# Input loads ahead of weights, half of the squares' sum on GpSimd, and an earlier sigmoid table

## The chip, the core and the metric

One core of a Trainium2 chip runs the whole program. TensorE (PE) multiplies matrices into PSUM, VectorE (DVE), ScalarE (ACT) and GpSimd (POOL) work on elements, and SyncE (SP) issues the DMA loads and stores. Each engine takes its instructions in the order written, and semaphores order the engines among each other. The metric is the device time of one execution in microseconds, the median of several runs. Before the change it is 633.22 us (three runs, 632.15 to 635.92).

## The reference

Two layers of a streaming encoder over 544 positions (512 of a prompt, 32 of a sample with a past). In layer 0 the input x is normalised by its root mean square, projected, gated and convolved:

```
u = x * rsqrt(mean(x*x) + eps) * g_pre
a, gl, z = split(u @ w_in, 3);  v = a * sigmoid(gl)
y = silu(layernorm(depthwise_conv(v, 31 taps)))
h = x + rmsnorm((y * silu(z)) @ w_out) * g_post
```

Layer 1 is a latent attention (low-rank q, a shared latent for keys and values, 16 heads, block-causal mask), again gated and projected. Everything is float32. The kernel reaches float32 accuracy in its projections with three matmuls per product: each operand is split into a rounded high part and the low rest, and high x high, high x low and low x high are summed.

The change touches only the start of layer 0: the loads, the norm of x, and the ScalarE table for the first sigmoid.

## The kernel before

**Layout.** x is held as xT: 1024 channels in 8 tiles of 128 partitions, 544 positions as columns. The columns are two halves of 272, called half 0 and half 1 (`blk(0)`, `blk(1)`). "Tile n" is channel tile n mod 8 of half n div 8, so there are 16 of them.

**Loads.** SP issues x in four quarters (half 0 in two, half 1 in two), each of 4 channel tiles, and the weights in units of 128 x 384 through a ring of 5 stage buffers. Unit u + 5 is loaded once GpSimd has finished unit u (`lo_done`).

**Weights.** ScalarE rounds a unit to its high part (`hi`, L406), and GpSimd subtracts it to get the low part (`lo`, L412).

**The norm, half by half.** ScalarE squares x into y, two tiles at a time (`xsquare`, L515). VectorE adds the eight square tiles up in four folds (`xfold`, L854): three of two tiles each, a last one of a single tile. TensorE multiplies by ones to sum over the partitions (`xstat`, L1429). VectorE makes the variance (L860), ScalarE the root (`sqrt_of`, L521), VectorE the reciprocal (L871).

**The scaled tiles.** For n = 0 to 15 VectorE writes x * g * reciprocal into PSUM (L911, semaphore `u_full`), ScalarE rounds it to the high part (L537, `uhi_done`), and VectorE subtracts for the low part (L892, `u_lo`), one tile behind. The program puts the folds of half 1 into this loop at n = 0 and n = 1, its variance at n = 6 and its reciprocal at n = 8.

**The first products.** TensorE takes tile n as soon as its low part is there: six matmuls (gate and value columns, three each; L421 to L423). The sum for half 1 stands in its stream in front of the products of tile 4. After tile 15 ScalarE takes the sigmoid of the gate columns (L592); TensorE's next group, 48 matmuls, writes into the same PSUM banks and waits for it. Then VectorE multiplies value and sigmoid (`glu`, L927 and L928) and works off the taps of the convolution (L952 to L957), one channel group j after another. The second `glu`, for j = 1, stands among the taps of j = 0 and needs the second group of TensorE matmuls of j = 1.

**Tables.** ScalarE holds one table of functions at a time. The first instruction loads the one with the square root. The next load before the change is the one that the first sigmoid needs, and it stands right in front of it.

The order of all this is fixed by the order in which each engine's program is written; no scheduler moves anything.

Of the kernel before, what the change touches and what calls it, by code (L numbers as in the profile page):

```python
# [196 lines left out]
def build(nc, x_t, state_t, ckv_t, ckr_t, w_in, w_ao, w_kv, w_bi, w_qb, w_kb, w_bo, vecs_d, cc_d, ss_d, krs_d,  # L197
          y_out, conv_out, c_out, kr_out):
    ctx = ExitStack()
    with ctx:  # L200
        def sem(name):
            return ctx.enter_context(nc.semaphore(name))
# [101 lines left out]
        tap_done, y_ready = sem("tap_done"), sem("y_ready")  # L304
        ln_norm, yz_full = sem("ln_norm"), sem("yz_full")
        h_done, xn_full, xn_lo_dve = sem("h_done"), sem("xn_full"), sem("xn_lo_dve")
        xsum_done = sem("xsum_done")
        osum_done, hsum_done, qsum_done, fsum_done = sem("osum_done"), sem("hsum_done"), sem("qsum_done"), sem("fsum_done")
        kr_done, c_full, qn_full = sem("kr_done"), sem("c_full"), sem("qn_full")
        g_evac_dve, rope_done, max_done, prob_done, pt_evac_dve, att_done = (  # L310
# [15 lines left out]
        def blk(b):  # L326
            return slice(b * HB, (b + 1) * HB)
# [104 lines left out]
        def _(sp):  # L432
# [5 lines left out]
            for i in range(4):  # L438
                b, k = i // 2, KD // 2 * (i % 2)
                sp.dma_start(xT[:, k:k + KD // 2, blk(b)], x_t[:, k:k + KD // 2, blk(b)]).then_inc(x_in[i], 16)  # L440
                if i == 1:
                    for u in range(3):
                        load(u)
            sp.dma_start(vecs[:], vecs_d).then_inc(vecs_in, 16)
            for u in range(3, 8):
                load(u)
            sp.dma_start(state[:], state_t).then_inc(state_in, 16)
            for j in range(KD):
# [55 lines left out]
        def _(act):  # L504
# [19 lines left out]
                xsquare(n)  # L524
            hi(act, 0)
            hi(act, 1)
            sqrt_of(N_IN, 0)
            xsquare(4)
            xsquare(5)
            hi(act, 2)  # L530
            hi(act, 3)
            xsquare(6)
            xsquare(7)
            for n in range(2 * KD):
                b, k = divmod(n, KD)
                act.wait_ge(u_full, n + 1)
                nc.scalar.activation(act_hi[:, k, blk(b)], ps[:, 6 + n % 2, 0:HB], ACT.Copy).then_inc(uhi_done, 1)  # L537
                if n < 4:
                    hi(act, 4 + n)
                if n >= KD:  # L540
                    hi(act, n)
                if n == 6:
                    sqrt_of(N_IN + 1, 1)

            def ysquare(j):

# [290 lines left out]
        def _(dve):  # L837
# [34 lines left out]
                dve.wait_ge(rstd_done, n + 1)  # L872


            def xfold(b, i):

                if i < 4:
                    fold(y[:, 0:2, blk(b)], y[:, 2 * i:2 * i + 2, blk(b)], xsq_done, 4 * b + i + 1, xsum_done,
                         4 * b + i - 1 if i > 1 else 0)
                else:  # L880
                    fold(y[:, 0, blk(b)], y[:, 1, blk(b)], xsq_done, 4 * b + 4, xsum_done, 4 * b + 3)

            for i in range(1, 5):
                xfold(0, i)
            dve.wait_ge(xstat_done, 1)
            variance(N_IN, ps[:, 4, 0:HB], D, 0)
            inverse(N_IN, None, 0)
# [7 lines left out]
            dve.wait_ge(vecs_in, 16)  # L895
            for n in range(2 * KD):
                b, k = divmod(n, KD)
                if n == 0:
                    xfold(1, 1)
                    xfold(1, 2)  # L900
                if n == 1:
                    xfold(1, 3)
                    xfold(1, 4)
                if n == 6:
                    dve.wait_ge(xstat_done, 2)
                    variance(N_IN + 1, ps[:, 5, 0:HB], D, 1)
                if n == KD:
                    inverse(N_IN + 1, None, 1)
                if n >= 2:
                    dve.wait_ge(u_lo, n - 1)  # L910
                nc.vector.scalar_tensor_tensor(out=ps[:, 6 + n % 2, 0:HB], in0=xT[:, k, blk(b)],  # L911
                                               scalar=vecs[:, V_PRE0 + k:V_PRE0 + k + 1],
                                               in1=stat(N_IN + b), op0=ALU.mult, op1=ALU.mult).then_inc(u_full, 1)
                if n:
                    u_split(n - 1)
# [356 lines left out]
        def _(pool):  # L1272
            nc.gpsimd.memset(eye, 0.0).then_inc(pool_set, 1)
            pool.wait_ge(pool_set, 1)
            nc.gpsimd.affine_select(out=eye, in_=eye, compare_op=ALU.not_equal, fill=1.0, base=0,
                                    pattern=[[-1, P]], channel_multiplier=1).then_inc(pool_set, 1)
            for u in range(2 * KD):
                lo(pool, u)

            def tap_add(j, i):  # L1280

# [136 lines left out]
        def _(pe):  # L1418
# [6 lines left out]
            pe.wait_ge(const_set, 1)  # L1425

            def xstat(b):
                pe.wait_ge(xsum_done, 4 * (b + 1))
                nc.tensor.matmul(ps[:, 4 + b, 0:HB], ones[:], y[:, 0, blk(b)], start=True, stop=True).then_inc(xstat_done, 1)  # L1429

            xstat(0)
# [1 line left out]
            for j in range(KD):  # L1433
                if j == 0:
                    for b in range(NB):
                        for k in range(KD):
                            if b == 0:
                                ready(pe, k)
                                if k == 4:
                                    xstat(1)  # L1440
                            pe.wait_ge(u_lo, KD * b + k + 1)
                            for t in range(2):
                                last = mm3(half_of(t, b), cols(slot(k), P * t), act_hi[:, k, blk(b)],
                                           act_lo[:, k, blk(b)], k == 0, k == KD - 1)
                                if b and k == KD - 1:
                                    last.then_inc(mt_done, 1)
# [373 lines left out]
```

## Time and profile before

| what | us |
|---|---|
| median of 3 runs | 633.22 (632.15 to 635.92) |
| profiled execution | 633.14 |
| its span | 631.4 |
| TensorE busy | 545.7 (86%) |
| VectorE busy | 451.3 (71%) |
| ScalarE busy | 306.8 (49%) |
| GpSimd busy | 298.2 (47%) |

The profiled execution is told by the device; the span is the time from the first to the last instruction that the profile shows, so 1.74 us lie outside it. Busy shares are means over stages with different limits: which engine sets the pace is seen from the table by stages and from what ended each wait.

### The profile page before, as it was taken

To read this page: it belongs to the slowest core of one execution; us is meant where nothing else is said; L and a number is where in the kernel's file an instruction comes from. 1 tells how busy PE (TensorE), PEld (TensorE's weight loads), DVE (VectorE), ACT (ScalarE), POOL (GpSimd) and SP (SyncE) were. 2 spreads that over 40 slices of the span, in tenths; PEclk is the share of its full clock that TensorE was granted. 3 is DMA by queue.
4 is the path that set the end of the run, shared out by engine and by line. 5 is a ranking of instruction groups with operands and counts; after the bars stand their busy time and mean duration, and the time that the engine had idled before them with its cause. 6 is when DMAs were issued, how large, how long until landed. Compare 5 with 4: busy or idle time off the path is not lost.

```text
span 631.4 us, 10827 instructions
## 1 busy us (share of the span) xinstructions
PE 545.7 (86%) x4044; PEld 497.4 (79%) x4044; DVE 451.3 (71%) x855; ACT 306.8 (49%) x730; POOL 298.2 (47%) x271
## 2 busy tenths in 40 slices
PE   0699999999983669998999998998999999779981
PEld 0699999988952669987999997777777777469980
DVE  4887999999987994888758122856867868850066
ACT  5454665365646773655336325355454554444230
POOL 3349878898894770473647731102111112205033
PEclk9999999999997689999999999999999999959996
DMA  7233133222430310332133222020030031101003
GB/s 239 82 104 89 52 103 90 79 76 66 136 86 1 103 31 28 88 95 67 34 101 105 95 83 57 15 72 17 13 91 2 17 120 36 49 17 51 2 30 112
DMA packets 31397, 43.17 MB, mean 68 GB/s; under 512 B 5840, under 2 KB 21744, under 8 KB 31344
## 3 DMA queue, kind: packets, MB, share of 16 engines
q1 hardware_dynamic: 31344, 42.47, 23.2%
q8 instruction: 32, 0.52, 0.4%
q14 instruction: 21, 0.17, 0.1%
HBM read 37.25 MB, written 3.10 MB: 64 GB/s over the span
## 4 chain that ended last, share of the span: by engine, by line
PE 42%; DVE 36%; ACT 6%; issue 5%; POOL 4%; SPq 3%; DMA 3%; DVEq 0%; ACTq 0%; POOLq 0%
DVE ps L957 13%; PE ps L421 10%; PE ps L423 9%; PE ps L422 9%; PE ps L1636 3%; PE ps L1677 2%; DVE probs L1209 2%; POOL part L1288 2%; DVE y L1002 2%; PE ps L1657 2%; DVE ps L871 2%; SPq L484 2%; ACT probs L787 2%; POOL rlow_lo L412 1%; DVE y L854 1%
## 5 line engine op out<-in xcount | busy, mean ns | idle before, releaser
L412 POOL TENSOR_TENSOR rlow_lo<-stage,rlow_hi 128x384 fp32r<-128x384 f32 (+2 forms) x88 | 99.6, 1141 | 215.8 <-ACT rlow_hi L406 215.8
L421 PE MATMUL ps<-act_hi,rlow_hi 128*128 128x272 f32 (+1 forms) x368 | 110.7, 301 | 22.0 <-POOL act_lo L1341 9.3
L957 DVE SCALAR_TENSOR_TENSOR ps<-v,vecs,ps 128x574 f32<-128x574 f32 x165 | 120.6, 814 | 0.0
L421 PE MATMUL ps<-act_hi,rtop_hi 128*128 128x272 f32 x384 | 112.8, 294 | 7.7 <-ACT zs L627 4.0
L423 PE MATMUL ps<-act_hi,rtop_lo 128*128 128x272 f32 x384 | 111.7, 291 | 0.0
L422 PE MATMUL ps<-act_lo,rtop_hi 128*128 128x272 f32 x384 | 111.3, 290 | 0.0
L423 PE MATMUL ps<-act_hi,rlow_lo 128*128 128x272 f32 (+1 forms) x368 | 107.9, 293 | 0.0
L422 PE MATMUL ps<-act_lo,rlow_hi 128*128 128x272 f32 (+1 forms) x368 | 107.8, 293 | 0.0
L421 PEld LDWEIGHTS ps<-act_hi,rlow_hi 128*128 128x128 f32 (+1 forms) x368 | 70.4, 191 | 25.6 <-POOL act_lo L1341 10.6
L421 PEld LDWEIGHTS ps<-act_hi,rtop_hi 128*128 128x128 f32 x384 | 73.0, 190 | 9.1 <-ACT zs L627 4.3
L412 POOL TENSOR_TENSOR rtop_lo<-stage,rtop_hi 128x384 fp32r<-128x384 f32 (+1 forms) x56 | 64.8, 1177 | 28.4 <-ACT rtop_hi L406 28.4
L422 PEld LDWEIGHTS ps<-act_lo,rtop_hi 128*128 128x128 f32 x384 | 73.1, 190 | 0.1
L423 PEld LDWEIGHTS ps<-act_hi,rtop_lo 128*128 128x128 f32 x384 | 72.9, 190 | 0.0
L422 PEld LDWEIGHTS ps<-act_lo,rlow_hi 128*128 128x128 f32 (+1 forms) x368 | 70.5, 192 | 0.2
L423 PEld LDWEIGHTS ps<-act_hi,rlow_lo 128*128 128x128 f32 (+1 forms) x368 | 70.3, 191 | 0.0
L787 ACT ACTIVATE probs<-ps,negmax 128x128 f32<-128x128 f32 (+4 forms) x68 | 35.1, 521 | 46.4 <-DVE negmax L1186 46.2
L1288 POOL TENSOR_TENSOR part<-prod,part 128x574 f32<-128x574 f32 x41 | 54.2, 1323 | 0.6
L406 ACT ACTIVATE rlow_hi<-stage 128x384 fp32r<-128x384 f32 (+2 forms) x88 | 46.7, 550 | 7.2 <-DMA stage<-w_in 2.3
L560 ACT ACTIVATE prod<-v,vecs 128x574 f32<-128x574 f32 x57 | 42.8, 766 | 7.9 <-POOL part L1288 4.9
L1636 PE MATMUL ps<-kT,qT 100*128 100x128 f32 (+3 forms) x128 | 41.1, 442 | 2.1 <-DMA qT<-rope_r 2.1
L1677 PEld LDWEIGHTS ps<-pT,vt 128*64 128x64 f32 x320 | 18.3, 144 | 23.8 <-ACT pT L797 12.7
L406 ACT ACTIVATE rtop_hi<-stage 128x384 fp32r<-128x384 f32 (+1 forms) x56 | 30.6, 561 | 12.0 <-DVE stage L398 9.5
(180 smaller groups left out, 1254.9 us busy)
## 6 DMA issues: line engine op xcount, KB each, us to landing
stage<-w_in SPq DMA_DIRECT2D x64, 192.0 KB, 2.7
stage<-w_bi SPq DMA_DIRECT2D x24, 256.0 KB, 2.7
stage<-w_ao SPq DMA_DIRECT2D x16, 256.0 KB, 2.9
stage<-w_bo SPq DMA_DIRECT2D x16, 256.0 KB, 2.7
stage<-w_qb SPq DMA_DIRECT2D x16, 192.0 KB, 2.6
xT<-x_t SPq DMA_DIRECT2D x4, 544.0 KB, 5.5
y_out<-xT SPq DMA_DIRECT2D x16, 136.0 KB, 1.8
stage<-w_kb SPq DMA_DIRECT2D x8, 256.0 KB, 2.6
```

What stands on the lines that cost most here:

```text
L406: nc.scalar.activation(slot(u)[0], stage[:, u % STAGES, 0:unit_cols(u)], ACT.Copy).then_inc(hi_done, 1)
L412: nc.gpsimd.tensor_tensor(l, stage[:, u % STAGES, 0:unit_cols(u)], h.bitcast(F32), ALU.subtract).then_inc(lo_done, 1)
L421: nc.tensor.matmul(out, wh, xh, start=start, stop=False)
L422: nc.tensor.matmul(out, wh, xl, start=False, stop=False)
L423: return nc.tensor.matmul(out, wl, xh, start=False, stop=stop)
L484: sp.dma_start(qT[NOPE + 16 * half:NOPE + 16 * half + 16, h, :], rope_r[64 * half + 16 * i:64 * half + 16 * i + 16, g % 2, :]).then_inc(ro ...
L560: nc.scalar.activation(prod[:, i % PRODS, :], v[:, j % 2, w:w + CCOLS], ACT.Copy, scale=vecs[:, V_DW + WIDTH * j + w:V_DW + WIDTH * j + w ...
L787: last = nc.scalar.activation(probs[:, i % 2, e, 0:n], ps[:, 2 * (i % 2) + e, 0:n], ACT.Exp, bias=negmax[:, i % 2, e:e + 1], scale=SCALE, ...
L957: ins = nc.vector.scalar_tensor_tensor(out=dst, in0=src, scalar=tap, in1=dst, op0=ALU.mult, op1=ALU.add)
L1288: nc.gpsimd.tensor_tensor(p, prod[:, i % PRODS, :], prod[:, 0, :] if i == 1 else p, ALU.add).then_inc(padd_done, 1)
L1636: nc.tensor.matmul(ps[:, bank, 0:n], qT[0:QK, h, q:q + P], kT[0:QK, h, 0:n], start=True, stop=True).then_inc(scores_done, 1)
L1677: last = nc.tensor.matmul(ps[64 * e:64 * e + 64, out_bank(i), 0:P], vt[:, v0 + t, col:col + VH], pT[:, e, P * t:P * t + P], start=t == 0, ...
```

## The change

Four edits, all at the start of the program.

1. SP issues the third quarter of x (first half of half 1) ahead of the weights, then two weight units instead of three, then the last quarter.
2. The folds of half 1 go from VectorE to GpSimd, where they stand behind the low parts of weight units 1 and 2 (two folds behind each). They count on a semaphore of their own, `xsum1_done`.
3. ScalarE's first two squares of half 1 go ahead of the first root, and the other two ahead of weight units 2 and 3. TensorE's sum for half 1 goes from tile 4 to tile 2, the variance on VectorE from n = 6 to n = 5.
4. A one-element activation with the sigmoid (`load_table`) stands behind the second root.

```
@@ SP
-                if i == 1:
-                    for u in range(3):
+                if i == 2:
+                    for u in range(2):
                         load(u)
             sp.dma_start(vecs[:], vecs_d).then_inc(vecs_in, 16)
-            for u in range(3, 8):
+            for u in range(2, 8):
                 load(u)
@@ ScalarE
             hi(act, 1)
-            sqrt_of(N_IN, 0)
             xsquare(4)
             xsquare(5)
+            sqrt_of(N_IN, 0)
+            xsquare(6)
+            xsquare(7)
             hi(act, 2)
             hi(act, 3)
-            xsquare(6)
-            xsquare(7)
...
                 if n == 6:
                     sqrt_of(N_IN + 1, 1)
+                    load_table(ACT.Sigmoid)
@@ VectorE
-                if n == 0:
-                    xfold(1, 1)
-                    xfold(1, 2)
-                if n == 1:
-                    xfold(1, 3)
-                    xfold(1, 4)
-                if n == 6:
+                if n == 5:
                     dve.wait_ge(xstat_done, 2)
                     variance(N_IN + 1, ps[:, 5, 0:HB], D, 1)
@@ GpSimd
+            def xfold1(i):
+                pool.wait_ge(xsq_done, 4 + min(i + 1, 4))
+                if i > 1:
+                    pool.wait_ge(xsum1_done, i - 1)
+                if i < 4:
+                    nc.gpsimd.tensor_tensor(y[:, 0:2, blk(1)], y[:, 0:2, blk(1)], y[:, 2 * i:2 * i + 2, blk(1)],
+                                            ALU.add).then_inc(xsum1_done, 1)
+                else:
+                    nc.gpsimd.tensor_tensor(y[:, 0, blk(1)], y[:, 0, blk(1)], y[:, 1, blk(1)], ALU.add).then_inc(xsum1_done, 1)
             for u in range(2 * KD):
                 lo(pool, u)
+                if u in (1, 2):
+                    xfold1(2 * u - 1)
+                    xfold1(2 * u)
@@ TensorE
-                pe.wait_ge(xsum_done, 4 * (b + 1))
+                pe.wait_ge(xsum1_done if b else xsum_done, 4)
...
-                                if k == 4:
+                                if k == 2:
                                     xstat(1)
```

How the order of instructions moves at three places. VectorE from the reciprocal of half 0 on, before the change (y<-y are folds of half 1, ps<-xT a scaled tile, act_lo a low part):

```order
L871 RECIPROCAL ps<-var_b 128x272
L854 TENSOR_TENSOR y<-y 128x2x272 x2
L911 SCALAR_TENSOR_TENSOR ps<-xT,vecs,ps 128x272
L854 TENSOR_TENSOR y<-y 128x2x272
L854 TENSOR_TENSOR y<-y 128x272
L911 SCALAR_TENSOR_TENSOR ps<-xT,vecs,ps 128x272
L892 TENSOR_TENSOR act_lo<-ps,act_hi 128x272
```

The same place on VectorE with the change:

```order
L872 RECIPROCAL ps<-var_b 128x272
L899 SCALAR_TENSOR_TENSOR ps<-xT,vecs,ps 128x272 x2
L886 TENSOR_TENSOR act_lo<-ps,act_hi 128x272
L899 SCALAR_TENSOR_TENSOR ps<-xT,vecs,ps 128x272
L886 TENSOR_TENSOR act_lo<-ps,act_hi 128x272
```

The four folds are gone from between the reciprocal and the first low part. GpSimd with the change, over the low parts of weight units 0 to 7 (before, the eight low parts stood there alone):

```order
L412 TENSOR_TENSOR rlow_lo<-stage,rlow_hi 128x384 [waits hi_done] x2
L1271 TENSOR_TENSOR y<-y 128x2x272 [waits xsq_done]
L1271 TENSOR_TENSOR y<-y 128x2x272 [waits xsum1_done,xsq_done]
L412 TENSOR_TENSOR rlow_lo<-stage,rlow_hi 128x384 [waits hi_done]
L1271 TENSOR_TENSOR y<-y 128x2x272 [waits xsum1_done,xsq_done]
L1274 TENSOR_TENSOR y<-y 128x272 [waits xsum1_done,xsq_done]
L412 TENSOR_TENSOR rlow_lo<-stage,rlow_hi 128x384 [waits hi_done] x5
```

The low parts of units 2 to 7 now stand behind two or four folds. ScalarE over the first root, as one piece of the difference (y<-xT are squares, rlow_hi roundings of weights, var_b the root):

```order
 L406 ACTIVATE rlow_hi<-stage 128x384 x2
-L521 ACTIVATE var_b<-var_b 128x272
 L515 ACTIVATE y<-xT 128x2x272 x2
-L406 ACTIVATE rlow_hi<-stage 128x384 x2
+L521 ACTIVATE var_b<-var_b 128x272
 L515 ACTIVATE y<-xT 128x2x272 x2
+L406 ACTIVATE rlow_hi<-stage 128x384 x2
```

Two squares of half 1 moved in front of the root, the other two in front of the roundings of units 2 and 3.

## Rows read from the trace of the kernel before

**Rows 1.** Windows: start:end, us, busy PE, PEld, DVE, ACT, POOL, granted clock, DMA, GB/s.

```profile
16.66:24.50 7.84, 5.26 (x25) 5.29 (x26) 5.72 (x14) 4.04 (x10) 4.04 (x4) 1.00 0.46 126
36.70:57.20 20.50, 19.65 (x156) 19.43 (x155) 13.95 (x20) 11.50 (x21) 11.17 (x11) 1.00 0.28 81
57.20:163.00 105.80, 101.97 (x808) 101.31 (x807) 104.71 (x160) 55.10 (x108) 93.19 (x84) 1.00 0.30 84
```

**Rows 2.** Timeline of VectorE: start us, us, instruction, count, [idle before, releaser].

```profile
12.18 1.86 DVE L871 RECIPROCAL ps<-var_b 128x272 f32<-128x272 f32 x1 [0.49 <-ACT var_b L521]
14.08 2.66 DVE L854 TENSOR_TENSOR y<-y 128x544 f32<-128x544 f32 x2
16.66 0.49 DVE L911 SCALAR_TENSOR_TENSOR ps<-xT,vecs,ps 128x272 f32<-128x272 f32 x1
...
18.66 0.43 DVE L892 TENSOR_TENSOR act_lo<-ps,act_hi 128x272 fp32r<-128x272 f32 x1
...
25.13 0.44 DVE L860 TENSOR_SCALAR var_b<-ps 128x272 f32<-128x272 f32 x1 [2.50 <-PE ps L1429]
...
29.02 0.51 DVE L911 SCALAR_TENSOR_TENSOR ps<-xT,vecs,ps 128x272 f32<-128x272 f32 x1
...
29.90 0.51 DVE L911 SCALAR_TENSOR_TENSOR ps<-xT,vecs,ps 128x272 f32<-128x272 f32 x1
...
57.22 0.69 DVE L927 TENSOR_TENSOR v<-ps,sig 128x512 f32<-128x512 f32 x1 [4.53 <-PE ps L423]
```

**Rows 3.** Timeline of TensorE (sums of squares are L1429, products L421 to L423).

```profile
9.96 1.25 PE L1429 MATMUL ps<-y,ones 128*128 128x272 f32 x2 [9.96 <-DVE y L854]
19.24 0.56 PE L421 MATMUL ps<-act_hi,rlow_hi 128*128 128x272 f32 x1 [8.03 <-POOL rlow_lo L412]
...
22.10 0.43 PE L421 MATMUL ps<-act_hi,rlow_hi 128*128 128x272 f32 x1
...
24.47 0.62 PE L1429 MATMUL ps<-y,ones 128*128 128x272 f32 x2
...
30.01 0.36 PE L421 MATMUL ps<-act_hi,rlow_hi 128*128 128x272 f32 x1 [1.66 <-DVE act_lo L892]
...
37.22 0.28 PE L423 MATMUL ps<-act_hi,rlow_lo 128*128 128x272 f32 x1
...
38.73 0.39 PE L421 MATMUL ps<-act_hi,rlow_hi 128*128 128x272 f32 x1 [0.85 <-ACT sig L592]
```

**Rows 4.** Timeline of ScalarE.

```profile
4.94 1.20 ACT L515 ACTIVATE y<-xT 128x544 f32<-128x544 f32 x2 [2.64 <-DMA xT<-x_t]
6.42 1.20 ACT L515 ACTIVATE y<-xT 128x544 f32<-128x544 f32 x2 [0.28 <-DMA xT<-x_t]
...
11.72 0.43 ACT L521 ACTIVATE var_b<-var_b 128x272 f32<-128x272 f32 x1 [3.27 <-DVE var_b L860]
...
17.19 0.40 ACT L537 ACTIVATE act_hi<-ps 128x272 fp32r<-128x272 f32 x1 [2.03 <-DVE ps L911]
...
36.76 1.28 ACT L592 ACT_TABLE_LOAD   x1
38.05 0.62 ACT L592 ACTIVATE sig<-ps 128x544 f32<-128x544 f32 x1
```

**Rows 5.** Timeline of GpSimd, the low parts of weight units 0 and 1.

```profile
8.12 2.55 POOL L412 TENSOR_TENSOR rlow_lo<-stage,rlow_hi 128x384 fp32r<-128x384 f32 x2 [6.59 <-ACT rlow_hi L406]
```

**Rows 6.** Chain of waits, the last fold of half 0: start us, us, what.

```profile
8.77 1.06 DVE y L854
```

**Rows 7.** Groups by shape on GpSimd: count | busy us, mean ns | idle before, releaser.

```profile
L412 POOL TENSOR_TENSOR rlow_lo<-stage,rlow_hi 128x384 fp32r<-128x384 f32 x48 | 49.8, 1043 | 119.1 <-ACT rlow_hi L406 119.1
...
L1341 POOL TENSOR_TENSOR act_lo<-y,act_hi 128x272 fp32r<-128x272 f32 x16 | 13.9, 873 | 16.0 <-ACT act_hi L632 15.9
...
L1305 POOL TENSOR_TENSOR ysums<-y,ysums 128x544 f32<-128x544 f32 x5 | 6.9, 1373 | 0.0
...
L1341 POOL TENSOR_TENSOR c_lo<-cf,c_hi 128x544 fp32r<-128x544 f32 x2 | 3.6, 1842 | 0.0
```

More of the change, by code:

```diff
@@ L306, in build @@
         h_done, xn_full, xn_lo_dve = sem("h_done"), sem("xn_full"), sem("xn_lo_dve")
-        xsum_done = sem("xsum_done")
+        xsum_done, xsum1_done = sem("xsum_done"), sem("xsum1_done")
         osum_done, hsum_done, qsum_done, fsum_done = sem("osum_done"), sem("hsum_done"), sem("qsum_done"), sem("fsum_done")
@@ L872, in inverse @@
                 dve.wait_ge(rstd_done, n + 1)
[L875 to L884, printed above, removed]
+            for i in range(1, 4):
+                fold(y[:, 0:2, blk(0)], y[:, 2 * i:2 * i + 2, blk(0)], xsq_done, i + 1, xsum_done, i - 1 if i > 1 else 0)
+            fold(y[:, 0, blk(0)], y[:, 1, blk(0)], xsq_done, 4, xsum_done, 3)
             dve.wait_ge(xstat_done, 1)
```

## The prediction

> **What bounds the kernel now.** I read the table of stages first, then the chain of waits, and last each engine's timeline over the opening 57 us. From 57.2 to 163 us VectorE works 104.7 of 105.8 us [rows 1]: the taps of the convolution set the pace, and what follows starts from their end. VectorE enters that stretch late. Its second gate (L927) waits 4.53 us for TensorE and starts at 57.22 [rows 2]. TensorE, in turn, is busy 19.65 of the 20.5 us before that [rows 1], from the matmul at 38.73 that waited for the first sigmoid [rows 3]. So the end of the kernel hangs on the moment that sigmoid is done (38.05 + 0.62) [rows 4], and everything later is counted from it: if it comes x earlier, the end comes x earlier. That is the one lever; GpSimd and ScalarE busy time elsewhere costs nothing here.
>
> The path to the sigmoid, in order: x lands, ScalarE squares, VectorE folds, TensorE sums (9.96), variance, root, reciprocal (12.18) [rows 2, 3]. Then VectorE folds half 1, two folds from 14.08 and two more behind the first scaled tile, and the first product starts at 19.24 [rows 2, 3]. The trace names GpSimd as releaser there; the program shows that this product needs weight tile 0, long there, and the first low part (VectorE, 18.66 + 0.43 = 19.09 [rows 2]), so I take VectorE. Then four steps of products, the sum for half 1 (24.47), the variance (25.13) before scaled tile 6, the reciprocal, scaled tile 8 at 29.02, and eight tiles at VectorE's pitch of 0.88 (29.02 to 29.90) [rows 2, 3].
>
> **The change part by part.** The sum is made against the profiled execution, 633.14 us (span 631.40 and 1.74 around it), 0.08 below the median of 633.22.
>
> *Load order.* x quarters 0 and 1 stay first, so the first squares stay at 4.94 [rows 4]. Landings follow issue order: the last fold of half 0 needs quarter 1, and a quarter takes about 1.5 us (first square of quarter 0 at 4.94, of quarter 1 at 6.42 [rows 4]). Quarter 2 now lands at about 7.9, and weight 0, a third of its size, at about 8.4. Its rounding is done near 8.9, so the first low part on GpSimd starts near 9.0, not 8.12 [rows 5]. The last fold of half 0 took 1.06 from 8.77 on [rows 6], while that subtraction ran (8.12 to about 9.4 [rows 5]); a VectorE operation on 272 columns without that company takes 0.43 [rows 2]. At 8.77 it now gets in ahead: -0.6 for all that follows (bounds: 0, if the weight lands sooner, and -0.6).
>
> *Squares of half 1 ahead of the root.* Two squares (1.20 the pair) now stand before the root on ScalarE, which was idle 3.27 before it [rows 4]: nothing. The other two, after the root, end near 12.7.
>
> *Folds off VectorE.* Four folds leave, 2.66 us of them ahead of the first scaled tile [rows 2]. That scaled tile starts right behind the reciprocal, 14.08 for 16.66. Its high part follows at +0.53 (16.66 to 17.19 [rows 2, 4]) and takes 0.40, the low part 0.43, and 0.15 passes before the matmul: the first product starts at 14.08 + 0.53 + 0.44 + 0.43 + 0.15 = 15.63 for 19.24.
>
> *Sum of half 1 at tile 2.* Twelve matmuls stand ahead of it, 22.10 - 19.24 = 2.86 us at the pitch of a fresh start [rows 3], so it can begin at 18.49. That pitch, about 0.23 us for 272 columns, and the 0.43 that a matmul lasts in it are those of the 1.2 GHz level; it came after eight idle microseconds, and by 24.47 it was gone, although the granted clock reads 1.00 over the whole stretch [rows 1, 3]. The sum took 1.25 at that level (9.96) and 0.62 at the upper one (24.47) [rows 3]. The variance began 0.66 after the start of the faster one [rows 2, 3], so it begins 1.29 after the start of a slower one. I take the lower level: variance at 18.49 + 1.29 = 19.78 for 25.13, which is -5.35. It now stands one tile earlier, so one more scaled tile and low part (0.88) lie between it and the reciprocal: +0.88.
>
> *The folds on GpSimd.* No row shows them. Nearest: an add of 544 columns, all operands in SBUF, 1.37; below it 1.04 at 384 columns; above it 1.84, a subtraction of 544 columns; for 272 columns 0.87 [rows 7]. I take 1.37, the same operation and size. GpSimd: low parts 0 and 1 (1.04 each) from 9.0 to 11.1, two folds to 13.9 (the second waits for a square at about 12.1), low part 2 to 15.0, two folds (1.37 + 0.87) to 17.2. TensorE, 0.6 earlier by the first item, reaches the sum at 17.9. So the folds are covered by 0.7 us; at 1.84 each, with low parts of 1.27 (2.55 for two [rows 5]), they end at 19.4, 1.5 late.
>
> *Behind those folds* on GpSimd stand the low parts of weights 2 to 7, and on SP's queue the loads of weights 7 to 12, each waiting for one. Were it 3 us from the end of low part 2 to the landing of weight 7 (18.0), ScalarE would round it about 0.9 late at tile 3, but VectorE then waits for the variance until 19.2: nothing. Low parts 3 to 7 end by about 22.6, and the step for tile 7 starts near 25.
>
> *Sigmoid table.* The load (1.28) sat between the last rounding and the sigmoid: 36.76 to 38.05 [rows 4]. The matmul group it needs ends at 37.22 + 0.28 = 37.50 [rows 3], so only 0.50 comes back. In its new place, after the second root, the load (1.28 [rows 4]) and a one-element dummy run from about 21.7 to 23.2; tile 7's high part ends at 23.6, and VectorE, busy with the reciprocal (1.86 [rows 2]), wants it at 24.4: nothing, with 0.8 to spare.
> The Trainium skill ("ScalarE: Activation LUTs", What ACT_TABLE_LOAD costs) puts a switch at about 1.28 of load and 1.38 of drain. This trace has the 1.28, and the sigmoid starting at its end, without the drain. By the page the switch would overrun its cover by about 0.6 and the time would be 628.2.
>
> **Sum:** -0.6 - 5.35 + 0.88 - 0.50 = -5.57 at the sigmoid, so 633.14 - 5.57 = **627.6 us**. The stall of 4.5 us before the second gate stays: both sides of it move together.
>
> **The rivals.** *GpSimd sets the second sum.* With 1.84 folds it starts 1.5 late: 629.1. For: two of the folds wait for squares that now come after the root. Against: that 1.84 row is another operation, and the add says 1.37 [rows 7].
>
> *TensorE stays at its lower level.* An idle gap of about 1.5 us before tile 7 remains. If half 1 ran at 0.23 per matmul, each step of six would take 1.38 for 0.88: 8 x 0.5 = 4.0, giving 631.6. Against: TensorE idled 1.66 before 30.01, and the matmuls after it still last 0.28, not 0.43 [rows 3].
> The Trainium skill ("TensorE: Matmul & The Clock Gate", Part 1) says that the default is the lower clock and recent activity lifts it; the rise between 22.10 and 24.47, after idling and then steady work, agrees, and by that rule sparser products would pay this price.
>
> *The gain is lost later.* Beyond 163 us I have taken for granted that all shifts; were something there paced by other work than the taps, up to all would vanish: 630 to 633. Against: weights, GpSimd's adds and the stores are all released by gates or by matmuls that shift too, and nothing runs to a time of its own.
>
> *Slower: TensorE blocked at tile 2.* The sum waits in order, ahead of all later products. Were GpSimd's in-place add of two strided tiles three times dearer (4.1 a fold), its chain would end near 27, the sum 9.2 late: 636.8. It decides from 3.2 us per fold on (5.6 late). No GpSimd row of this size is over 1.84 [rows 7].
>
> *It does not do what it says.* The order of instructions shows the table load gone from the sigmoid and four adds on GpSimd, so I give this nothing beyond the cases above.
>
> **How the numbers follow.** Forecast 0.66, own range 626.2 to 628.9; GpSimd-bound 0.15; lower clock 0.05; lost later 0.10; blocked 0.04. Upward, the lock (0.6) and the GpSimd bound (1.5) give 629.7, and I reach into the later cases to 631.0. Downward, the sum of half 1 at the upper level gives -0.6, and the lowest run before lies 1.07 under its median: 625.9. A difference of 1% (6.33 us) is about what a measurement of this kernel tells from no change. Faster by that needs 626.9 or less, 0.7 beyond the forecast: about a third of the forecast's cases, 0.24. Slower by it needs 639.5, so only a part of the blocked case: 0.02. The rest, 0.74, is within 1%.
>
> **What the profile would show.** Right: the last fold of half 0 at 0.44; first product near 15.0; second sum at about 17.9 and 1.25 long; variance near 19.2; sigmoid near 32.5 with no load before it; second gate near 51.7. Wrong: GpSimd folds over 1.8, a wait of TensorE for them, ScalarE late behind the table load, or VectorE idle longer than 4.5 us before its second gate.

## The result, and the profile after

The new kernel takes **630.46 us** (median of 15 runs, 628.90 to 631.84), the old one in the same session 635.76 (15 runs, 631.89 to 637.27). The ratio is 0.9934 with a 95% interval of 0.9919 to 0.9950: faster, by 0.5 to 0.8%, which is 3.2 to 5.1 us of 635.76. It is not the quotient of the two medians, which differ by 5.30 (0.9917): the old kernel's runs spread over 5.4 us, the new one's over 2.9. The forecast was 627.6. The profiled executions are 633.14 before and 630.3 after (span 628.6), 2.84 apart, although the second gate comes 5.63 earlier.

The front went as forecast. VectorE's timeline of the new kernel (start us, us, instruction, count, [idle before, releaser]):

```profile
7.21 2.10 DVE L855 TENSOR_TENSOR y<-y 128x544 f32<-128x544 f32 x3 [0.26 <-ACT y L515]
10.74 0.44 DVE L861 TENSOR_SCALAR var_b<-ps 128x272 f32<-128x272 f32 x1 [1.43 <-PE ps L1431]
11.68 1.86 DVE L872 RECIPROCAL ps<-var_b 128x272 f32<-128x272 f32 x1 [0.50 <-ACT var_b L521]
13.57 0.91 DVE L899 SCALAR_TENSOR_TENSOR ps<-xT,vecs,ps 128x272 f32<-128x272 f32 x2
...
19.13 0.44 DVE L861 TENSOR_SCALAR var_b<-ps 128x272 f32<-128x272 f32 x1 [1.50 <-PE ps L1431]
...
51.59 0.69 DVE L915 TENSOR_TENSOR v<-ps,sig 128x512 f32<-128x512 f32 x1 [4.53 <-PE ps L423]
```

Against [rows 2]: the scaled tiles begin at 13.57 for 16.66, the variance of half 1 at 19.13 for 25.13 (forecast 19.2), the second gate at 51.59 for 57.22 (forecast 51.7), with the same 4.53 idle ahead of it. The last fold of half 0, behind the group at 7.21, takes 0.44 (8.87 to 9.31) for the 1.06 of [rows 6].

TensorE's timeline of the new kernel, its two sums and the first product:

```profile
9.46 1.25 PE L1431 MATMUL ps<-y,ones 128*128 128x272 f32 x2 [9.46 <-DVE y L855]
15.13 0.57 PE L421 MATMUL ps<-act_hi,rlow_hi 128*128 128x272 f32 x1 [4.43 <-DVE act_lo L886]
...
17.99 1.11 PE L1431 MATMUL ps<-y,ones 128*128 128x272 f32 x2
```

Against [rows 3]: first product 15.13 for 19.24 (forecast 15.0), second sum 17.99 for 24.47 (17.9), 1.11 long (1.25), with no idle time ahead of it: GpSimd is not late. GpSimd's timeline, whose first low parts now start at 9.13 for the 8.12 of [rows 5], says by how much:

```profile
9.13 1.99 POOL L412 TENSOR_TENSOR rlow_lo<-stage,rlow_hi 128x384 fp32r<-128x384 f32 x2 [7.59 <-ACT rlow_hi L406]
11.09 2.81 POOL L1271 TENSOR_TENSOR y<-y 128x544 f32<-128x544 f32 x2
13.85 0.99 POOL L412 TENSOR_TENSOR rlow_lo<-stage,rlow_hi 128x384 fp32r<-128x384 f32 x1
14.80 1.35 POOL L1271 TENSOR_TENSOR y<-y 128x544 f32<-128x544 f32 x1
16.29 0.77 POOL L1274 TENSOR_TENSOR y<-y 128x272 f32<-128x272 f32 x1
```

The folds take 1.35 to 1.41 (1.37 taken from [rows 7]) and end at 17.06, 0.9 before the sum starts. ScalarE's timeline has the table load in its new place and none ahead of the sigmoid ([rows 4]):

```profile
21.64 1.28 ACT L506 ACT_TABLE_LOAD   x1
22.93 0.20 ACT L506 ACTIVATE warm<-ones 1x1 f32<-1x1 f32 x1
...
32.42 0.62 ACT L593 ACTIVATE sig<-ps 128x544 f32<-128x544 f32 x1 [0.83 <-PE ps L423]
```

So 5.6 us reach the second gate. The rest of the study is about what happens to them afterwards. I matched the two traces instruction by instruction and read the lead of the new kernel along the span (us; the column 186 is GpSimd's add at 186.29, the last one the end of the span):

```
at, us in the old kernel       60    186    206    285    385    420    470    560    600    end
new against old             -5.63  -5.36  -3.97  -3.74  -3.71  -3.15  -2.95  -2.91  -3.79  -2.84
```

The lead is lost in jumps. The largest, 1.39 at 200 us, is in the channel sums behind the convolution. TensorE's timelines, old kernel first:

```profile
199.65 0.72 PE L1478 MATMUL ps<-y,ones 128*128 128x272 f32 x2 [2.08 <-DVE y L975]
200.22 0.62 PE L1478 MATMUL ps<-ysums,ones 128*128 128x272 f32 x2
200.68 0.62 PE L1478 MATMUL ps<-y,ones 128*128 128x272 f32 x2
```

```profile
194.29 1.28 PE L1480 MATMUL ps<-y,ones 128*128 128x272 f32 x2 [2.08 <-DVE y L963]
195.36 1.11 PE L1480 MATMUL ps<-ysums,ones 128*128 128x272 f32 x2
196.27 1.05 PE L1480 MATMUL ps<-y,ones 128*128 128x272 f32 x2
```

The same three sums last 1.28, 1.11 and 1.05 for 0.72, 0.62 and 0.62. The windows of the old and of the new kernel over them (start:end, us, busy PE, PEld, DVE, ACT, POOL, granted clock, DMA, GB/s):

```profile
198.20:204.80 6.60, 2.56 (x10) 1.82 (x10) 5.04 (x13) 1.64 (x5) 0.00 (x0) 1.00 0.00 1
```

```profile
187.00:197.00 10.00, 5.77 (x12) 3.98 (x13) 5.76 (x12) 5.59 (x11) 4.56 (x4) 0.50 0.00 0
```

The granted clock is 1.00 there before and 0.50 after: the 2.4 and the 1.2 GHz level. In both kernels TensorE idles for over 5 us, sums for 3 us and idles 2.08 more ahead of these sums; both fall to the lower level there, and in the old kernel's profiled execution it had ended when the sums began. The jump of 0.95 at the end of the span is of the same kind: eight matmuls of the last sums take 2.10 at the upper level before, 3.07 after, where the level fell at 613.6 (old kernel, then new):

```profile
616.37 2.10 PE L1713 MATMUL ps<-fsq,ones 128*128 128x272 f32 x8 [2.32 <-DVE fsq L854]
```

```profile
612.58 3.07 PE L1715 MATMUL ps<-fsq,ones 128*128 128x272 f32 x8 [2.32 <-DVE fsq L855]
```

So the first theory (**A**): the whole gain reaches the end, less or more what the clock level does in each execution. Its rival (**B**): something tied to the change takes part of the gain back.

### The profile page after: what moved, and what is told of

Read it like the earlier page. It is cut to its first block, busy times and chain, and to the rows that moved or that the text cites. A ratio compares the mean times of both kernels' runs of the same rounds, so it can differ in the third digit from the quotient of the medians.

```text
span 628.6 us, 10828 instructions
## 1 busy us (share of the span) xinstructions
PE 546.4 (87%) x4044; PEld 497.4 (79%) x4044; DVE 447.7 (71%) x851; ACT 306.9 (49%) x731; POOL 301.1 (48%) x275
## 4 chain that ended last, share of the span: by engine, by line
PE 48%; DVE 32%; ACT 5%; issue 5%; POOL 3%; SPq 3%; DMA 2%; DVEq 0%; ACTq 0%; POOLq 0%
PE ps L421 12%; PE ps L423 11%; PE ps L422 11%; DVE ps L945 11%; PE ps L1638 3%; PE ps L1679 2%; DVE probs L1197 2%; POOL part L1290 2%; DVE y L990 2%; PE ps L1659 2%; DVE ps L872 2%; ACT probs L788 2%; SPq L484 1%; DVE rowmax L1170 1%; POOL rlow_lo L412 1%
## 5 line engine op out<-in xcount | busy, mean ns | idle before, releaser
L412 POOL TENSOR_TENSOR rlow_lo<-stage,rlow_hi 128x384 fp32r<-128x384 f32 (+2 forms) x88 | 97.8, 1123 | 211.6 <-ACT rlow_hi L406 211.6
L421 PE MATMUL ps<-act_hi,rlow_hi 128*128 128x272 f32 (+1 forms) x368 | 110.5, 300 | 17.4 <-POOL act_lo L1343 9.5
L421 PE MATMUL ps<-act_hi,rtop_hi 128*128 128x272 f32 x384 | 112.8, 294 | 7.7 <-ACT zs L628 4.0
L423 PE MATMUL ps<-act_hi,rtop_lo 128*128 128x272 f32 x384 | 111.7, 291 | 0.0
L423 PE MATMUL ps<-act_hi,rlow_lo 128*128 128x272 f32 (+1 forms) x368 | 107.6, 292 | 0.0
L421 PEld LDWEIGHTS ps<-act_hi,rlow_hi 128*128 128x128 f32 (+1 forms) x368 | 70.1, 191 | 20.9 <-POOL act_lo L1343 10.8
L421 PEld LDWEIGHTS ps<-act_hi,rtop_hi 128*128 128x128 f32 x384 | 73.0, 190 | 9.1 <-ACT zs L628 4.3
L423 PEld LDWEIGHTS ps<-act_hi,rtop_lo 128*128 128x128 f32 x384 | 72.9, 190 | 0.0
L423 PEld LDWEIGHTS ps<-act_hi,rlow_lo 128*128 128x128 f32 (+1 forms) x368 | 70.0, 190 | 0.0
L1679 PEld LDWEIGHTS ps<-pT,vt 128*64 128x64 f32 x320 | 17.7, 140 | 24.2 <-ACT pT L798 13.1
```

What stands on the lines that cost most here:

```text
L412: nc.gpsimd.tensor_tensor(l, stage[:, u % STAGES, 0:unit_cols(u)], h.bitcast(F32), ALU.subtract).then_inc(lo_done, 1)
L421: nc.tensor.matmul(out, wh, xh, start=start, stop=False)
L423: return nc.tensor.matmul(out, wl, xh, start=False, stop=stop)
L1679: last = nc.tensor.matmul(ps[64 * e:64 * e + 64, out_bank(i), 0:P], vt[:, v0 + t, col:col + VH], pT[:, e, P * t:P * t + P], start=t == 0, ...
```

## The experiments

**Parts of the change undone, one at a time.** All four start from the new kernel. e1:

```diff
-                    load_table(ACT.Sigmoid)
```

> The new kernel without the early load of the sigmoid table; all else as in it. Both theories of the front agree: the 1.28 us load stands again between the last rounding and the first sigmoid, of which 0.5 us is not covered by the matmul group, so the first sigmoid starts at about 32.9 for 32.42 and the second gate at about 52.1 for 51.59. Theory A (the whole gain at the gate reaches the end, and the rest varies from run to run with the places at which TensorE's granted level falls): 630.46 + 0.5 = 631.0. Theory B (what comes after the gate gives back about half of any shift): 630.7. Rival on the table itself (the early load delays the last high parts by as much as it saves): gate unchanged, 630.5.

e2 (the four adds leave GpSimd):

```diff
+                if n < 2:
+                    for i in (2 * n + 1, 2 * n + 2):
+                        ... fold i of half 1 on VectorE
-                if u in (1, 2):
-                    xfold1(2 * u - 1)
-                    xfold1(2 * u)
```

> The new kernel with the folds of half 1 back on VectorE, two ahead of the first scaled tile and two behind it; sum still at tile 2, loads and table as in the new kernel. The folds ahead of the first scaled tile cost it 2.66 us again, and those behind it about 1.0 more on VectorE: second gate at 54.9 to 55.4 for 51.59. Theory A: the end follows by the whole, 630.46 + 3.5 = 634.0. Theory B: by half, 632.2. Rival (the folds on GpSimd were not what mattered, the early sum was): gate later by under 1, 631.

e3:

```diff
-                if n == 5:
+                if n == 6:
...
-                                if k == 2:
+                                if k == 4:
```

> The new kernel with the sum of half 1 on TensorE at input tile 4 and its variance one scaled tile later, as before the change; folds still on GpSimd. Scaled tile 8 then waits for a sum that comes two tiles later (about 1.8), less the one tile (0.88) that no longer stands between variance and reciprocal: second gate about 0.9 later, 52.5. Theory A: 631.4. Theory B: 630.9. Rival (the sum at tile 2 costs TensorE a wait for GpSimd that tile 4 would hide): gate the same or earlier, 630.0 to 630.5.

e4:

```diff
-                if i == 2:
-                    for u in range(2):
+                if i == 1:
+                    for u in range(3):
```

> The new kernel with the old order of loads (weight 0 ahead of quarter 2 of x). The last fold of half 0 meets the low part of weight 0 on GpSimd again and takes about 1.06 for 0.43: second gate about 0.5 later, 52.1. Theory A: 631.0. Theory B: 630.7. Rival (the load order only moves weight 0 and changes nothing on the path): gate at 51.6, 630.5.

Measured, the gate in the profile, the median, and the ratio to the old kernel of that session (634.28):

```
     second gate   against 51.59   median    ratio [95%]
e1      51.83          +0.24       630.22    0.9950 [0.9931, 0.9969]
e2      55.77          +4.18       631.97    0.9953 [0.9933, 0.9973]
e3      52.70          +1.11       631.07    0.9953 [0.9937, 0.9970]
e4      52.60          +1.01       630.89    0.9956 [0.9937, 0.9975]
```

The signs are as forecast, the sizes only roughly: 0.24 for an expected 0.5 (e1), 4.18 for 3.3 to 3.8 (e2), 1.11 for 0.9 (e3) and 1.01 for 0.5 (e4). The large part is the adds' leaving VectorE: in e2 the 2.66 us of folds stand ahead of the first scaled tile again and the variance starts at 22.58:

```profile
13.57 2.66 DVE L855 TENSOR_TENSOR y<-y 128x544 f32<-128x544 f32 x2
...
22.58 0.44 DVE L861 TENSOR_SCALAR var_b<-ps 128x272 f32<-128x272 f32 x1 [1.35 <-PE ps L1434]
```

The four add up to 6.5, not 5.6: in e1, e2 and e4 TensorE's level rose, and then fell once more for the next products, which it did not in the new kernel's profile. Windows of e1:

```profile
18.30:25.00 6.70, 5.04 (x36) 4.56 (x35) 6.16 (x12) 2.43 (x7) 3.57 (x5) 1.00 0.51 147
25.10:28.40 3.30, 3.30 (x17) 3.30 (x16) 3.16 (x9) 3.03 (x8) 3.30 (x4) 0.50 0.30 81
```

So the gate of one execution is itself uncertain by some tenths. In the times e1, e3 and e4 cannot be told from the new kernel; e2 can, but it is only 1.5 later for 4.18 at the gate. That speaks for B, and it became a clue: matched with the old kernel, e2 keeps its lead unchanged through the places where the new kernel's lead drops (-1.45 at the gate, -1.49 at 186, -1.50 at 206, -1.49 at 285; further on it is -1.13 at 470 and -1.88 at the end).

**The clock level held up.** Matmuls of a block of ones, whose results nobody reads, fill TensorE's idle time behind the convolution, in the new kernel (e5) and in the old one (e6); in e7 and e8 also ahead of the first sums.

```diff
+            def awake(n, bank):
+                for _ in range(n):
+                    nc.tensor.matmul(ps[:, bank, 0:P], ones[:], ones[:], start=True, stop=True)
...
+            awake(16, 2)
             pe.wait_ge(fold_done, folds(KD - 2))
...
+            awake(24, 0)
             for k in range(KD):
                 pe.wait_ge(yz_lo, k + 1)
... and, in e7 and e8
+            awake(12, 3)
             xstat(0)
+            awake(12, 3)
```

> The new kernel with idle TensorE time behind the convolution filled by matmuls whose results nobody reads (16, 3, 24, 12 and 6 of them, in the gaps of 5.8, 2.1, 7.9, 4.1 and 2.3 us). Theory A (the stages behind the gate lose time only where TensorE's granted level falls, at places that differ from run to run): the level stays at 1.00 from 20 to about 550, each channel sum takes 0.62 instead of up to 1.28, and the end comes 1 to 2 us earlier: 628.4 to 629.4, with a narrower spread. Theory B (something else behind the gate takes back half of a shift): the level stays up and the end moves by less than 0.5. Rival C (the extra matmuls stand in order ahead of real ones and delay them): 631 or more.

> The kernel before with the same idle TensorE time filled by the same matmuls. This takes the fall of the clock level behind the convolution out of the comparison with the new kernel so filled. Theory A: this is later than it by the whole of the front, 5.6 +- 0.7, so 634 to 635. Theory B: by 2.8 to 3.5, 631.5 to 632.5.

> The new kernel with TensorE kept busy behind the convolution as above, and ahead of its first sums too: 12 matmuls before the sum of half 0, 12 between it and the first product, 4 in the gap of 1.67 us before input tile 7. Where the granted level has risen by 9.5, the first sum takes 0.62 for 1.25 (-0.6), and the twelve products ahead of the second sum go at half their pitch, so that this sum starts when the folds on GpSimd end (about 16.5) and takes 0.62: variance at 17.2 for 19.13, second gate at about 49.7 for 51.59. Time: 1.9 below the new kernel filled behind the convolution alone, about 627. Rival: the folds on GpSimd now set the sum and hold the gain to the 0.6 of the first sum (second gate 51.0). Rival: the level does not rise before the first product, gate unchanged at 51.6, and so does the time.

> The kernel before with the same matmuls in front and behind. First sum -0.6; the second sum, at tile 4, is held by VectorE's pitch of 0.88 per tile rather than by TensorE: variance about 1.5 to 2 earlier than 25.13, second gate at 55 to 55.5 for 57.22. Theory A: later than the new kernel so filled by what their gates differ, 5.3 to 5.8. Theory B: by half of that.

```
                      second gate   median (runs)   ratio to the old kernel [95%]
e5 new, tail             51.66       627.96 (6)     0.9898 [0.9873, 0.9923]
e6 old, tail             57.27       631.42 (10)    0.9942 [0.9924, 0.9961]
e7 new, front and tail   50.51       625.91 (5)     0.9872 [0.9847, 0.9897]
e8 old, front and tail   57.02       630.69 (8)     0.9947 [0.9927, 0.9967]
```

Idle TensorE time does cost this kernel: each version is faster with useless matmuls in it. (For e5 alone the interval still touches that of the new kernel, 0.9919 to 0.9950; e7's lies clear of it.) A window of e5 over the stretch shown above:

```profile
187.00:197.00 10.00, 5.65 (x21) 4.32 (x21) 5.81 (x12) 5.65 (x11) 4.64 (x4) 0.92 0.01 2
```

The level did not stay up throughout, as theory A had expected: it is at 0.50 from 195.4 to 198.8 and from 386.6 to 390.0 in e5, and from 195.0 to 198.4 and 389.5 to 392.9 in e6. So the two clocks are close, not the same.

Even so, theory A fell. With the tail filled in both, the new kernel leads by 631.42 - 627.96 = 3.46, B's number, for 5.61 at the gate; with the front filled too, 4.78 for 6.51. The lead of e5 over e6 still drops at 186, at 272 and at 453, by 0.28, 0.31 and 0.18, where their clocks agree. In e7 the second sum waits for GpSimd, [0.87 <-POOL], so the gate comes at 50.51 for the 49.7 expected: the folds had 0.9 to spare and no more. In e8 the level fell again from 17.4 to 24.2, and its gate moved by only 0.25 where 1.7 to 2.2 were expected.

```profile
17.32 0.70 PE L1436 MATMUL ps<-y,ones 128*128 128x272 f32 x2 [0.87 <-POOL y L1274]
```

**What takes a part of the rest: where an instruction stands in its engine's program.** At 186 us the drop begins on GpSimd. Its timelines, old kernel, then new:

```profile
184.95 1.20 POOL L1288 TENSOR_TENSOR part<-prod 128x574 f32<-128x574 f32 x1
186.29 4.10 POOL L1288 TENSOR_TENSOR part<-prod,part 128x574 f32<-128x574 f32 x3
```

```profile
179.31 1.20 POOL L1290 TENSOR_TENSOR part<-prod 128x574 f32<-128x574 f32 x1
180.94 4.10 POOL L1290 TENSOR_TENSOR part<-prod,part 128x574 f32<-128x574 f32 x3 [0.43 <-POOL part L1290]
```

The add starts 0.14 behind the one before it in the old kernel, 0.43 in the new one; the semaphore wait between them is long over, so the releaser named is nobody. VectorE's end of the taps waits for these adds. Counting each engine's records (instructions and waits) from 0, this add is number 196 on GpSimd in the new kernel. In the old one number 196 is a wait issued under a running add, and the same add is number 189: the change put seven records (four adds, three waits) ahead of it. On VectorE it took seven away. There the numbers of the other two drops are 447 and 703, 256 apart. In all ten profiles up to here, records 196 on GpSimd and 447 and 703 on VectorE are late whenever nothing covers them: 0.38 to 0.39, 0.40, and 0.21 to 0.22 behind their forerunners in the six with the new numbering; in the four with the old one they fall under other work. The same instructions under their old numbers start 0.09, 0.32 to 0.33 and 0.03 to 0.04 behind, so the stalls themselves are 0.30, 0.07 and 0.18. Theory **D**: a block of an engine's program begins there, and entering it costs 0.2 to 0.4 us. It is tested by one-element memsets at the start of the programs, where both engines idle: seven each in the new kernel (e11, and e9 with the tail filled), seven on GpSimd in the old one (e10).

```diff
+            for i in range(7):
+                nc.vector.memset(pad[:, i:i + 1], 0.0)
...
+            for i in range(7):
+                nc.gpsimd.memset(pad[:, 8 + i:9 + i], 0.0)
             nc.gpsimd.memset(eye, 0.0).then_inc(pool_set, 1)
```

> The new kernel with TensorE kept busy behind the convolution (as before), and with seven one-element memsets at the start of VectorE's program and seven at the start of GpSimd's, where both are idle; otherwise the same work. Theory D (an engine's instructions come in blocks of 128; where a block begins the engine stalls 0.2 to 0.4 us; the change shifted the numbering by seven on both engines and so moved three such stalls onto the path, at GpSimd's 196th instruction near 181 us and at VectorE's 447th and 703rd near 268 and 451): with the numbering shifted back on VectorE and on by seven on GpSimd, the three stalls are covered again, the lead over the old kernel so filled keeps its 5.6 through 181, 268 and 451 but for what the clock level takes, and the time is 0.7 to 0.8 below the same kernel without the memsets, 627.2 for 627.96. Rival (the three losses come from the clock or from transfers that do not move): they stay, 628.0. Second gate at 51.6 to 51.8 either way.

> The old kernel with seven one-element memsets at the start of GpSimd's program, nothing else. Theory D: its 196th instruction is now the add near 186.3 us (186.29 before), which starts 0.3 late; VectorE's end of the taps, near 197.1, comes 0.27 later against its second gate at 57.2, although the gate itself does not move. In the time this is 0.3 in 634.7, below what the runs can tell. Rival: no idle time ahead of that add.

> The new kernel with the fourteen memsets alone, TensorE left as it is. Theory D: the lead at the end of the taps is the full 5.6 instead of 5.36, no step at 268 and 451, time 0.7 to 0.8 below the new kernel, 629.7 for 630.46; the places of the lower clock level still differ from execution to execution. Rival: 630.5.

GpSimd's timelines at that add, e10 and then e11:

```profile
185.37 1.23 POOL L1291 TENSOR_TENSOR part<-prod 128x574 f32<-128x574 f32 x1
187.04 4.09 POOL L1291 TENSOR_TENSOR part<-prod,part 128x574 f32<-128x574 f32 x3 [0.44 <-POOL part L1291]
```

```profile
179.38 1.25 POOL L1295 TENSOR_TENSOR part<-prod 128x574 f32<-128x574 f32 x1
180.77 4.09 POOL L1295 TENSOR_TENSOR part<-prod,part 128x574 f32<-128x574 f32 x3
```

The stall goes where its number goes: seven memsets bring it into the old kernel (0.44) and take it out of the new one. VectorE's timeline at record 703, new kernel and then e11, shows the same, 0.22 ahead of the scaling and then nothing:

```profile
450.59 0.17 DVE L1194 RECIPROCAL rinv<-rowsum 128x2 f32<-128x2 f32 x1
450.97 0.88 DVE L1197 TENSOR_SCALAR probs<-probs,rinv 128x512 f32<-128x512 f32 x2 [0.22 <-DVE rinv L1194]
```

```profile
449.81 0.17 DVE L1197 RECIPROCAL rinv<-rowsum 128x2 f32<-128x2 f32 x1
450.01 0.88 DVE L1200 TENSOR_SCALAR probs<-probs,rinv 128x512 f32<-128x512 f32 x2
```

At record 447 the stall itself is small, but the two folds of `y` behind it take longer (new kernel, then e9):

```profile
268.38 2.26 DVE L855 TENSOR_TENSOR y<-y 128x544 f32<-128x544 f32 x2
```

```profile
265.83 2.02 DVE L858 TENSOR_TENSOR y<-y 128x544 f32<-128x544 f32 x2
```

GpSimd's timelines at the same place (new kernel, then e9) show a likely reason. The stall puts the first fold 0.03 behind the start of GpSimd's subtraction, and that fold takes 1.43; in e9 it starts 0.05 ahead of it and takes 0.72. It is the same company as that of the last fold of half 0 [rows 6].

```profile
268.35 0.88 POOL L412 TENSOR_TENSOR rlow_lo<-stage,rlow_hi 128x320 fp32r<-128x320 f32 x1 [0.53 <-ACT rlow_hi L406]
```

```profile
265.88 1.39 POOL L413 TENSOR_TENSOR rlow_lo<-stage,rlow_hi 128x320 fp32r<-128x320 f32 x1 [0.54 <-ACT rlow_hi L407]
```

The leads, matched as before:

```
at, us in the old kernel       60    186    206    285    385    420    470    560    600
e5 against e6               -5.61  -5.33  -4.41  -4.05  -4.09  -3.84  -3.62  -2.81  -2.83
e7 against e8               -6.51  -6.25  -6.25  -5.95  -5.70  -5.24  -5.06  -5.04  -4.24
e9 (with memsets) / e6      -5.65  -5.62  -4.96  -4.98  -4.99  -6.30  -6.30  -6.56  -7.99
e11 (with memsets) / old    -5.53  -5.53  -4.15  -4.21  -4.21  -3.91  -3.94  -4.13  -3.71
```

The three drops stand out best between e7 and e8, where nothing is lost at 200: 0.26 by 186, 0.30 at 272, 0.18 at 453. With the memsets the lead passes 186, 285 and 470 without them; what is left are jumps both ways at 200, 390 and behind 505. Those differ from execution to execution, and the profiled ones are not typical: e9's 624.02 is the fastest of its runs, those of e5, e6 and e11 (629.18, 632.03, 630.60) are the slowest.

The times lie on the expected side: e9 626.92 (6 runs; expected 627.2; ratio 0.9873 [0.9841, 0.9904]), e11 628.68 (6 runs; expected 629.7; ratio 0.9902 [0.9873, 0.9932]), e10 634.09 (0.9992 [0.9971, 1.0014], too small to be told, as expected). They do not show the memsets' worth by themselves: the intervals of e9 and e5 overlap, and so do those of e11 and the new kernel. The traces show it. One miss: e10's gate came 0.47 later, where I expected it not to move; at the taps' end the lag is 0.73, so the stall's share is 0.26.

The page of the profile lists two queues of kind instruction, one with 32 packets and 0.52 MB, some 16 KB each, and one with 21 packets and 0.17 MB, some 8 KB each. The Trainium skill ("Perfetto Trace Analysis", The 4-stage abstract model) says that an instruction has 64 bytes; a packet of 8 KB would then hold about 128 of them, an estimate, and 447 and 703 are two such blocks apart. Record 575, halfway, starts in the new kernel 0.08 before its forerunner ends, so no stall is seen there. The trace has the start of each packet: in the seven profiles with such stalls, a packet of the second queue starts 0.64 to 0.99 us behind the start of each late record. This ties the stalls to the loading of code. But these packets start after the late records have begun, so they are not what the engine waited for. What it does wait for stays open; the runs show that the stall sits at fixed numbers, moves with them and comes with such a packet.

**Everything together.** e12 is the new kernel with the memsets and with more of TensorE's idle time filled (18 and 12 matmuls in front; 24, 7, 30, 17, 10 and 10 behind).

> The fastest version that the runs so far point to: the new kernel with TensorE kept busy ahead of its first sums and in all idle gaps behind the convolution (18 and 12 in front, then 24, 7, 30, 17, 10 and 10), and the fourteen memsets. Against the one without the memsets (625.91): -0.75 by theory D, and -0.5 to -1.2 where the gaps near 188, 193 and 385 us are filled further, so 624.0 to 624.7. Rival (the added matmuls now overrun their gaps): 626 or more.

It takes **622.91 us** (5 runs, 622.45 to 624.21), ratio 0.9817 [0.9789, 0.9845]: below the expected 624.0, and 7.5 below the new kernel's median of another session. Its interval lies below e7's, but e12 also has more matmuls than e7, so the memsets' share of that is not told. The granted clock of each fortieth of the span on the page, new kernel and then e12:

```profile
PEclk9999999999996789999999998999999999969995
```

```profile
PEclk9999999999999999998999999999999999959996
```

## Why the prediction was right or wrong

*The front: right, term by term.* -0.6 for the last fold of half 0 (measured 0.44 for 1.06); variance at 19.13 for a forecast of 19.2; sigmoid at 32.42 for 32.5; the table load covered, with VectorE's reciprocal running beside it until 23.87; the sum 5.57 for a measured 5.63. The GpSimd-bound rival was off: the adds cost 1.35 to 1.41. The lower-clock rival was off in the profile shown; e1, e2 and e4 show that it can strike a few products in other executions.

*The step that failed* is the last one: "everything later is counted from it: if it comes x earlier, the end comes x earlier". I had given its failure 0.10, as the rival "the gain is lost later", with 630 to 633; it came to 630.46. How much is lost depends on where one looks: of 5.63 at the gate 2.84 is left in the two profiled executions; in the times 3.2 to 5.1 is left by the interval of the ratio, which does not contain the forecast's 5.57, and 5.30 by the medians. With the tails filled 3.46 of 5.61 is left, with the fronts filled too 4.78 of 6.51. My argument against that rival was that all later work is released by work that shifts too, and that "nothing runs to a time of its own". Two things were missing:

- *The number of an instruction.* The change moved 0.27 + 0.29 + 0.20 = 0.76 us of stalls (with the longer folds behind record 447) onto the path, at 186, 272 and 453 us, by shifting the numbering by seven on two engines. This part belongs to the change, is in all six profiles with the new numbering, and is shown by e9, e10 and e11. No row of the old kernel showed those stalls, since there each fell under other work.
- *TensorE's clock level behind the convolution.* In the two profiled executions the channel sums (1.39), the stage at 390 (0.56) and the last sums (0.95) lost, and the stage at 570 gained 0.88: 2.0 in sum. Holding the level up with useless matmuls takes 3.3 from the old kernel's median (634.71 to 631.42, one session) and 2.5 from the new one's (630.46 to 627.96, two sessions), so the level matters to both. That the change itself makes the level worse is not shown.

The stalls do not account for all that is lost in the times. Between e5 and e6 the medians lose 2.15, of which the stalls are 0.77; between e7 and e8 1.73, of which they are 0.74. And e2, which keeps the old numbering, is 1.5 slower than the new kernel for 4.18 at the gate: the stalls make 0.76 of the missing 2.7. The clock level and, in e5, the stretch near 506 us are the likely rest; no run shows it.

*The base was low.* I took 633.14 as what the old kernel takes. The median of later sessions is 634.28 to 635.76, with runs from 629.94 to 637.27: a spread of some 7 us, which three runs could not show. Of the 2.86 by which 627.6 was low, 2.62 is this base (635.76 in the new kernel's session), 0.76 the stalls, and -0.5 is a remainder that I put down to the clock level; no run shows it. So most of the miss in the number is the base, and the medians' 5.30 for 5.57 is in part luck: less the stalls alone it would be 4.8.

*The 1%.* "A difference of 1% (6.33 us) is about what a measurement of this kernel tells from no change" was too coarse: 15 runs of each told 0.66% from nothing. The chance of 0.74 for a change within 1% held, but what was measured is a gain, not the absence of one.

*Still open:* how often each execution meets the lower level at which stage; and why the attention's work near 506 us gave up 0.8 of e5's lead over e6, where the weights `w_bo` arrived later behind eight small transfers on the same queue (ScalarE idle 2.61 for 1.80). I did not follow it.

## What to carry to other kernels

Work moved between engines also moves every later instruction's number on both; if a lead shrinks in steps of 0.2 to 0.3 us and the releaser named has long been done, count the records to the late instruction in both traces, and try a few empty instructions at the start. Compare a lead along the whole span, instruction by instruction, before arguing from end times. Where TensorE idles ahead of short, critical matmuls, look at the granted clock of the stretch behind; filling the gap can be worth more than the change under study (here 622.91 for 630.46 together with the memsets).

## What the runs showed of the hardware

- GpSimd's record 196 starts 0.38 to 0.39 us behind its forerunner instead of 0.09 in each of the seven profiles in which it is an add on the path; VectorE's 703 starts 0.21 to 0.22 behind in the six in which it is a scaling on the path; the same scaling under another number starts 0.03 to 0.04 behind. In these profiles a packet of 8 KB on a queue of kind instruction starts 0.64 to 0.99 us behind each late record.
- The table load cost its 1.28 us and nothing more: the next ACTIVATE starts at 22.93, 0.01 behind its end.
- Matmuls of 128 columns of ones kept TensorE at the upper level from 6.0 to 541.9 us in e12, but for 279.1 to 282.5, and the first sum, 1.25 in the new kernel, took 0.72 there (0.73 in e7). The Trainium skill ("TensorE: Matmul & The Clock Gate", Part 1) says that the default is the lower clock and recent activity lifts it; e5, e7 and e12 agree.
